# Moving two large activation tensors 64 bytes down in SBUF, and two small tables from below them to above

## The reference, cut to what matters

```python
for l in range(DEPTH):                                   # 2 layers
    h = rms_norm(x, ln_g[l])
    proj = jnp.einsum('bsd,de->bse', h, w_in[l])         # q, k, v and gate columns of mixers A, B, C
    ...
    mix = jnp.concatenate([ya * silu(ga), yb * silu(gb), yc * silu(gc)], axis=-1)
    x = x + jnp.einsum('bse,ed->bsd', mix, w_out[l])
```

## The kernel before, in words

| tensor | first byte before | mod 512 before | after | mod 512 after |
|---|---|---|---|---|
| `half` (8 floats, exponent table of GpSimd's power) | 16,640 | 256 | 115,552 | 352 |
| `minus_one` (2 floats, written once, not read) | 16,672 | 288 | 115,584 | 384 |
| `act_hi` | 16,704 | 320 | 16,640 | 256 |
| `act_lo` | 65,856 | 320 | 65,792 | 256 |
| `sel_sb`, `rb_sb`, `rows_sb` (set-up of the bias tables, inside turned x) | | 320 | | 256 |
| `ident` | 115,008 | 320 | 114,944 | 256 |
| `sinks` | 115,520 | 320 | 115,456 | 256 |
| `x_sums` and everything above it | 115,616 | 416 | 115,616 | 416 |
| `w_hi`, `w_lo` | 131,136 and 141,376 | 64 | same | 64 |
| `x_cols`, `y`, `q_t`, `k_t`, `v_t`, `v_split`, `a_sum` | | 256 | same | 256 |
| `prob` (4 slots, 2064 bytes apart) | 190,208 | 256, 272, 288, 304 | same | same |
| `pt_hi`, `pt_lo`, `prob_t`, `a_part` | | 320 | same | 320 |

## Time and profile before

### The profile page before, as it was taken

How to read it: one execution, slowest core, us unless ns; L and a number is a source line. 1 busy time by engine, 2 the same in 40 slices (tenths; PEclk the granted TensorE clock), 3 DMA queues, 4 the chain that set the end, 5 groups by cost and what they waited for, 6 DMA issues and landing times.

```text
span 2838.6 us, 44181 instructions
## 1 busy us (share of the span) xinstructions
PE 2787.0 (98%) x14913; PEld 2498.6 (88%) x14913; DVE 1628.6 (57%) x3973; ACT 1226.1 (43%) x3017; POOL 928.5 (33%) x854
## 2 busy tenths in 40 slices
PE   8999999999999999999999999999999999999998
PEld 6888899989999999888788888999899999998887
DVE  3445644434676677577643465444357766775775
ACT  4322222225665566534542222222266654664443
POOL 0233433310464377500003333333105733774000
PEclk9999999998999999999999999999999999999999
DMA  4366656568444432374524565666674444325635
GB/s 172 97 186 195 189 183 187 174 180 220 135 130 119 129 102 81 123 257 126 192 89 131 178 196 170 192 186 192 182 217 128 108 126 135 90 73 180 214 122 174
DMA packets 419802, 444.25 MB, mean 157 GB/s; under 512 B 62487, under 2 KB 313015, under 8 KB 419580
## 3 DMA queue, kind: packets, MB, share of 16 engines
q1 hardware_dynamic: 419580, 441.44, 52.3%
HBM read 315.54 MB, written 125.80 MB: 155 GB/s over the span
## 4 chain that ended last, share of the span: by engine, by line
PE 89%; DVE 3%; issue 2%; POOL 2%; ACT 1%; DMA 1%; SPq 1%; DVEq 0%; ACTq 0%; POOLq 0%
PE bank L1402 14%; PE bank L1400 14%; PE bank L1401 14%; PE bank L1456 5%; PE bank L1458 5%; PE bank L1457 5%; PE bank L1433 5%; PE bank L1435 5%; PE bank L1434 5%; PE bank L1499 4%; PE bank L1526 3%; PE bank L1485 2%; PE bank L1486 2%; PE bank L1541 1%; PE bank L1542 1%
## 5 line engine op out<-in xcount | busy, mean ns | idle before, releaser
L1869 DVE TENSOR_TENSOR w_lo<-w_raw,w_hi 128x512 fp32r<-128x512 f32 x640 | 456.5, 715 | 463.7 <-ACT w_hi L1610 459.8
L1610 ACT CAST w_hi<-w_raw 128x512 fp32r<-128x512 f32 x640 | 395.4, 619 | 691.0 <-PE bank L1402 413.4
L1400 PE MATMUL bank<-w_hi,act_hi 128*128 128x512 f32 x1728 | 688.9, 399 | 1.4 <-DVE x_cols L2141 1.4
L1402 PE MATMUL bank<-w_hi,act_lo 128*128 128x512 f32 x1728 | 678.8, 393 | 0.0
L1401 PE MATMUL bank<-w_lo,act_hi 128*128 128x512 f32 x1728 | 677.3, 392 | 0.0
L2268 POOL TENSOR_SCALAR prob<-prob,denom 128x256 f32<-128x256 f32 (+2 forms) x288 | 345.2, 1203 | 291.0 <-DVE denom L2000 290.3
L1402 PEld LDWEIGHTS bank<-w_hi,act_lo 128*128 128x128 f32 x1728 | 372.4, 216 | 54.0
L1400 PEld LDWEIGHTS bank<-w_hi,act_hi 128*128 128x128 f32 x1728 | 373.2, 216 | 51.9 <-DVE x_cols L2141 1.9
L1401 PEld LDWEIGHTS bank<-w_lo,act_hi 128*128 128x128 f32 x1728 | 373.0, 216 | 48.5
L1456 PE MATMUL bank<-act_hi,w_hi 128*128 128x384 f32 x1024 | 347.7, 340 | 0.0
L1458 PE MATMUL bank<-act_hi,w_lo 128*128 128x384 f32 x1024 | 346.1, 338 | 0.0
(11 more groups left out here) (116 smaller groups left out, 4662.2 us busy)
## 6 DMA issues: line engine op xcount, KB each, us to landing
w_raw<-w_in SPq DMA_DIRECT2D x144, 512.0 KB, 4.5
w_sums<-sum_out SPq DMA_DIRECT2D x32, 1280.0 KB, 6.7
w_raw<-w_sums SPq DMA_DIRECT2D x80, 512.0 KB, 4.2
sum_in<-w_out SPq DMA_DIRECT2D x64, 512.0 KB, 5.7
heads_t<-turned SPq DMA_DIRECT2D x240, 128.0 KB, 2.4
q_t<-heads_t SPq DMA_DIRECT2D x192, 128.0 KB, 2.1
k_t<-keys_t SPq DMA_DIRECT2D x48, 384.0 KB, 5.7
w_raw<-w_out SPq DMA_DIRECT2D x32, 512.0 KB, 3.7
```

Of the source, the lines that this page charges most:

```text
L1400: pe.matmul(acc[t][:], hi, w_hi[:, n % W_RING, :], start=(k == 0), stop=False)
L1402: last = pe.matmul(acc[t][:], lo, w_hi[:, n % W_RING, :], start=False, stop=(k == KC - 1))
L1610: nc.scalar.copy(w_hi[:, n % W_RING, :], w_raw[:, load % W_RAW, j, :]).then_inc(w_hi_done, 1)
L1869: nc.vector.tensor_tensor(w_lo[:, n % W_RING, :], w_raw[:, load % W_RAW, j, :], w_hi[:, n % W_RING, :].bitcast(F32), ALU.subtract).then_in ...
```

## The change

The remainder at which turned x begins goes from 320 to 256 bytes; the two tables that lay in front of it (`half`, `minus_one`) are allocated behind `sinks` instead. `ln_cols` stays in front.

```diff
@@ -349,7 +349,7 @@
 X_LAG = 7
 KEEP_LAG = 5
-ROW_START = 320
+ROW_START = 256
@@ -593,8 +593,6 @@
         ln_cols = sb("ln_cols", [P, DEPTH * KC])
-        half = sb("half", [P, UPS])
-        minus_one = sb("minus_one", [P, 2])
         first = (top[0] - ROW_START + 511) // 512 * 512 + ROW_START
         top[0] = first
         act_hi = sb("act_hi", [P, KC, TOKENS], F32R)
@@ -611,6 +609,8 @@
         ident = sb("ident", [P, P])
         sinks = sb("sinks", [P, DEPTH * H_A])
+        half = sb("half", [P, UPS])
+        minus_one = sb("minus_one", [P, 2])
         x_sums = sb("x_sums", [P, TT, NS_OUT])
```

## The result

The median goes from 2838.49 us to 2846.74 us, 22 runs each (2832.50 to 2843.95, and 2839.24 to 2855.63). The ratio is 1.0028, with a 95% interval of 1.0020 to 1.0037: slower by 8.3 us, within the 0.3% that the prediction called no change, yet not zero.

The account below looks back on a forecast made before the run. TensorE, busy 98% of the span, was taken to bound the kernel. All terms summed to 0, so the profiled 2840.8 us stayed, stated as 2840 us, range 2829 to 2872.

Parts of the forecast that it names:

- no change: Whole kernel: time stays at 2840 us, with its own range 2832 to 2849; chance 0.48.
- the slower rival: Projection, L1400 to L1402: load and stream hinder each other at distance 192; 6 ns x 5184 = 31 us, 2871; chance 0.34.
- Only TensorE's reads can matter; weight loads by themselves, ScalarE, VectorE, GpSimd, `ident`, DMA: 0.: Whole kernel: addresses matter through TensorE's operand reads or by making it wait; each listed reader was costed at 0.
- Distance 192 in the projection: 0, taken over the row that pointed to 10 ns.: Projection's loads beside streams: bounded between 52 us more (10 ns x 5184) and 11.3 us gain, taken as 0.
- The two addresses slide past each other, so every distance comes up wherever they begin.: Contiguous slabs: the load reads 512 bytes, the stream more, so starting addresses do not matter; the argument for 0.
- Distance 320 costs nothing, by the transition of the earlier trace.: Gates: cost 0, since a weight piece loaded beside k_t at 320 showed 0.23 us, as in a steady row.
- Its case for the interleaved slabs: Interleaved slabs, where load and stream can keep one distance: if only these 1728 matmuls stay slow, 10 us, 2850.
- The faster rival: Interleaved slabs: the present distance is itself bad; up to -11.3 us, -15 with the DMA wait, so 2829; chance 0.18.
- DMA: 0, and an estimate of 2% of each load.: Loads into turned x's place: at most 4.0 us either way, taken as 0; aligned runs fetch 96 beats instead of 98.

Follow-up runs that it names:

- experiments 3 and 4: 3: kernel before with only half and minus_one moved to the end of SBUF, 2840.01 us; 4: changed kernel with ident back at 320, 2845.35 us.
- experiment 1: Changed kernel with w_raw, w_hi, w_lo also 64 bytes down, turned x at 256, small tables at the end; 2847.95 us, ratio 1.0029 to the kernel before.
- `s288`: Turned x at 320 as in the kernel before, w_hi and w_lo moved to 32; three contiguous slabs 209.28 us, three interleaved 211.44.
- `s320`: Turned x at 320 as in the kernel before, w_hi and w_lo moved to 0; three contiguous slabs 209.48 us, three interleaved 211.61.
- `s224`: Kernel before with w_hi and w_lo 32 bytes up, at 96; three contiguous slabs 209.34 us, three interleaved 211.86.
- experiment 2: Kernel before with 64 bytes left free ahead of w_raw, so weights at 128 and turned x still at 320; 2852.18 us, ratio 1.0044.

## Why the prediction was right or wrong

The forecast, no change to be told at 0.3%, held, and the time lies in its range; but one term of its sum was not zero, and the truth is a small case of the slower rival. That it held is luck of the address: at the distance of 128 (`s128`, the changed kernel with the weights 64 bytes further up) the two projections together take 19 us longer than before, not 10, and the reasoning of the prediction would have called that nothing as well.

- *Only TensorE's reads can matter; weight loads by themselves, ScalarE, VectorE, GpSimd, `ident`, DMA: 0.* Right. Loads stay at 188 and 309 ns, ScalarE and VectorE at 509 and 551, the power at 1755, and experiments 3 and 4 take out the tables and `ident`.
- *Distance 192 in the projection: 0, taken over the row that pointed to 10 ns.* Wrong, and this is the step that failed. It measured 10.05 us, or 1.9 ns on each of 5184, some 9 of them repeatable. The one row at this distance had the right sign; it was set aside because its load was for a transpose.
- *The two addresses slide past each other, so every distance comes up wherever they begin.* Wrong: the sweep finds 226.7 ns against 233.3 and 233.4 in the steady rows for 32 bytes of shift either way.
- *Distance 320 costs nothing, by the transition of the earlier trace rows.* Right for the gates (434.01 and 433.93 us in the stretch that holds most of them), wrong as a general reading: the output product lost 6.3 ns a matmul at 320 in experiment 1, with 512 columns in a long row. A single transition, read to a hundredth of a microsecond, says little of a steady row.
- *The slower rival: place, mechanism and point of decision.* The place is the one that the runs show, and so is the mechanism as far as it says that the spacing depends on how load and stream stand to each other. Its price was taken from the disturbed matmuls behind a turn, 6 ns. That is near what most distances cost in the contiguous slabs (5.1 to 5.4 ns over the whole slabs in `s288`, `s320`, `s128`, `s224`, 6.6 to 6.8 in their steady rows); the change landed on the exception. Its case for the interleaved slabs, where the two reads travel side by side, did not single them out: they lost 2.2 ns a matmul, the contiguous ones 1.4. At 1.9 ns it passed the 1.6 ns named as deciding by a little, and the median moved by 8.3 us, just short of 8.5.
- *The faster rival: the interleaved slabs suffer from their distance.* Wrong: no distance tried brings them below 210.47 us, nor the steady contiguous row below 226.7 ns. That their step is what makes them slower is then the reading left over; no run changed the step.
- *DMA: 0, and an estimate of 2% of each load.* The total holds. By the medians the 2% cannot be told here: from issue to landing they are 6.7 to 7.1 us in the four kernels with turned x at 256, and 7.0 to 7.5 in the eight with it at 320.

The Trainium skill's "SBUF — State Buffer", section "Who interferes with whom", says that TensorE has two independent read ports and never waits on anyone; the measurement decides against it where these are TensorE's own two reads. By it experiments 1 and 2 should have changed nothing, and experiment 1 moved the output product from 227.0 to 233.3 ns a matmul, experiment 2 the steady row of the projection from 226.7 to 228.8.

Why a period of 256 bytes, and why 192 is cheap for unit steps and dear for steps of 8 and 16 bytes, stays open, and so does where the two reads meet. No run here shows the inside of SBUF.

## What to carry to other kernels

Where a load of a stationary tile runs beside a matmul's stream, place the two tensors so that their first bytes agree mod 256; in a steady row of 512-column matmuls with a float32 load before each, that is worth up to 6.8 ns in 227 here, and any small table added in front can undo it. Check it with the start distance in a steady row, or with a window from one start to another, and not with the length of a window that one has chosen. And when one tensor is moved, count every pair that it and its neighbours take part in: experiment 1 mended one product and spoilt another.

## What was not expected of the hardware

- The cost depends on the distance of two addresses, and within what was tried it repeats every 256 bytes: three slabs take 204.85 us at 256 and at 0, and 209.3 to 209.5 at 32, 64 and 224 (mod 256).
- It is closely repeatable: two kernels with different tensors at different places but one distance have slabs of 206.05 and 206.04, 212.37 and 212.37 us. What the distance does not settle is small: 204.54 against 204.85 us at 256, and 208.78 against 209.32 at 384 and 128.
- It does not add up by pairs: one stream in three at a bad distance costs 3.77 us, all three 4.49.
- The gates, which stream 384 columns, hardly care (the stretch is 434.0 us at a distance of 256 and 433.9 at 320), while 512-column rows do. Their mean start distance at full clock is 176.2 ns before and 175.7 after, and 174.6 in `s320`, where the change of the weights puts the gates at 192: what is best for one stage need not be best for the next.
